# Turning the feed-forward activations outside TensorE: blocks on VectorE, an exchange by ScalarE

## The reference

```python
def swiglu_ffn(x, w_gu, w_down):
    a, u = jnp.split(x @ w_gu, 2, axis=-1)
    return (jax.nn.silu(a) * u) @ w_down

x = layer_norm(DEEPNORM_ALPHA * x + 0.5 * swiglu_ffn(x, ffn1_w_gu[l], ffn1_w_down[l]), ln1_g[l], ln1_b[l])
```

## Time and profile before

| | us |
|---|---|
| median of three runs | 1330.7 (1329.37, 1330.7, 1332.88) |
| span of the profiled execution, first to last instruction | 1328.9 |
| PE busy in it | 1311.6 |
| DVE busy | 1019.8 |
| ACT busy | 675.3 |
| POOL busy | 105.4 |

### The profile page before, as it was taken

One profiled execution on the slowest core, in us unless ns is written; L12 is line 12 of the kernel. 1 busy time (PEld: TensorE's weight loads), 2 busy tenths in 40 slices (PEclk: granted clock), 3 DMA queues, 4 the chain that ended last, 5 costly groups with the idle time before them and its releaser, 6 DMA issues.

```text
span 1328.9 us, 18838 instructions
## 1 busy us (share of the span) xinstructions
PE 1311.6 (99%) x7096; PEld 1110.0 (84%) x7096; DVE 1019.8 (77%) x1625; ACT 675.3 (51%) x1069; POOL 105.4 (8%) x153
## 2 busy tenths in 40 slices
PE   9999999999999999999999999999999999999997
PEld 7888888788888888888887888888889998798995
DVE  6677778887777677777787887778676798966986
ACT  6444444644444344444446545444436667457672
POOL 1010100011011001111010011111000000000000
PEclk9999999999999999999999999999999999999999
DMA  8977756527767656776646358777646473463630
GB/s 268 326 232 229 226 187 208 142 96 246 244 228 233 222 185 219 223 236 228 236 161 202 102 173 292 231 253 235 221 142 200 146 237 129 143 214 118 203 128 32
DMA packets 195049, 264.92 MB, mean 199 GB/s; under 512 B 17232, under 2 KB 140240, under 8 KB 194448
## 3 DMA queue, kind: packets, MB, share of 16 engines
q1 hardware_dynamic: 183248, 223.12, 52.1%
q0 software_dynamic: 11712, 40.60, 8.9%
HBM read 262.61 MB, written 1.07 MB: 198 GB/s over the span
## 4 chain that ended last, share of the span: by engine, by line
PE 87%; DVE 7%; DMA 4%; ACT 1%; issue 1%; SPq 0%; DVEq 0%; ACTq 0%
PE ps L818 26%; PE ps L820 26%; PE ps L819 26%; PE ps L902 4%; DVE w_lo L1317 2%; DMA w_raw<-in_ffn_w_gu 2%; PE ps L1049 2%; DMA w_raw<-in_w_in 1%; PE ps L1084 1%; PE ps L1110 1%; DVE few_first L1346 1%; ACT w_hi L1141 1%; DVE y L1345 1%; PE ps L1018 0%; PE ps L1096 0%
## 5 line engine op out<-in xcount | busy, mean ns | idle before, releaser
L1317 DVE TENSOR_TENSOR w_lo<-w_raw,w_hi 128x1024 fp32r<-128x1024 f32 (+2 forms) x420 | 496.9, 1213 | 128.5 <-ACT w_hi L1141 126.5
L1141 ACT ACTIVATE w_hi<-w_raw 128x1024 fp32r<-128x1024 f32 (+2 forms) x420 | 431.0, 1053 | 247.9 <-DMA w_raw<-in_ffn_w_gu 122.0
L818 PE MATMUL ps<-w_hi,col_hi 128*128 128x512 f32 (+2 forms) x1024 | 396.7, 387 | 3.6 <-DVE w_lo L1324 1.4
L820 PE MATMUL ps<-w_hi,col_lo 128*128 128x512 f32 (+2 forms) x1024 | 392.0, 383 | 0.0
L819 PE MATMUL ps<-w_lo,col_hi 128*128 128x512 f32 (+2 forms) x1024 | 391.9, 383 | 0.0
L818 PEld LDWEIGHTS ps<-w_hi,col_hi 128*128 128x128 f32 x1024 | 192.6, 188 | 44.0 <-DVE w_lo L1317 4.3
L820 PEld LDWEIGHTS ps<-w_hi,col_lo 128*128 128x128 f32 x1024 | 192.5, 188 | 38.2
L819 PEld LDWEIGHTS ps<-w_lo,col_hi 128*128 128x128 f32 x1024 | 192.5, 188 | 34.6
L818 PE MATMUL ps<-w_hi,lat_hi 128*128 128x512 f32 (+2 forms) x544 | 208.8, 384 | 0.0
L820 PE MATMUL ps<-w_hi,lat_lo 128*128 128x512 f32 (+2 forms) x544 | 206.5, 380 | 0.0
L819 PE MATMUL ps<-w_lo,lat_hi 128*128 128x512 f32 (+2 forms) x544 | 206.3, 379 | 0.0
(11 more groups left out here) (148 smaller groups left out, 1172.8 us busy)
## 6 DMA issues: line engine op xcount, KB each, us to landing
w_raw<-in_ffn_w_gu SPq DMA_DIRECT2D x352, 256.0 KB, 4.5
w_raw<-in_w_in SPq DMA_DIRECT2D x108, 512.0 KB, 4.6
w_raw<-in_ffn_w_down SPq DMA_DIRECT2D x88, 512.0 KB, 4.9
mod<-in_w_ada POOLq DMA_DIRECT2D x32, 768.0 KB, 7.6
w_raw<-in_w_out SPq DMA_DIRECT2D x24, 512.0 KB, 4.5
norm_g<-in_ln_g POOLq DMA_DIRECT2D x8, 512.0 KB, 4.2
norm_b<-in_ln_b POOLq DMA_DIRECT2D x8, 512.0 KB, 6.1
w_raw<-in_w_out SPq DMA_DIRECT2D x16, 256.0 KB, 4.5
```

The source lines that it names most:

```text
L818: pe.matmul(dst, a_hi, b_hi, start=start, stop=False)
L820: return pe.matmul(dst, a_lo, b_hi, start=False, stop=stop)
L1141: act.activation(half_of(w_hi[j], n, h), half_of(raw[j], n, h), ACT.Copy).then_inc(hi_ready, 1)
L1317: tt(half_of(w_lo[j], n, h), half_of(raw[j], n, h), half_of(w_hi[j], n, h).bitcast(F32), ALU.subtract)\
```

## The change

The job `ht` is kept for the last round alone (round 10). For rounds 0 to 9 of each feed-forward stage it becomes three jobs:

- `hturn:r`, behind `gu:r:1`: VectorE transposes the 32x32 blocks of `hidden` (128x512 in one instruction) into a new buffer `h_blocks`. A block's contents are turned then, but it lies in the wrong group of 32 partitions.
- `hmove:r`, in the middle of `gu:r+1:1` (`hmove:0` of stage 0 stands just ahead of `gu:1:1`; that of stages 2, 3 and 5 in the middle of `gu:2:0`, so that round 2 holds two): ScalarE copies the 16 pieces of 32 partitions x 128 columns to where they belong, into a new buffer `h_cols`.
- `hparts:r`, behind `gu:r+2:0` (for round 9: in the tail, behind `down:7:0`): ScalarE copies the high part to `lat_hi` in two instructions of 128x256, VectorE subtracts in two.

`h_blocks` and `h_cols` have two buffers each. `down:r` waits for `hparts:r` instead of `ht:r`, and `hidden` may be overwritten when `hturn` of two rounds before is done. The core of the diff:

```diff
+    blocks, moved, parts = (lambda r, kind=kind: [(kind, s, r)] for kind in ("hturn", "hmove", "hparts"))
...
     for r in range(2, ROUNDS):
-        jobs += gu(r, 0) + [("ht", s, r - 1)]
+        jobs += gu(r, 0)[:1] + (moved(0) if r == 2 and s > 0 else []) + stored(r - 1) + gu(r, 0)[1:] + parts(r - 2)
...
-        jobs += gu(r, 1)
+        jobs += gu(r, 1)[:1] + moved(r - 1) + gu(r, 1)[1:]
+        if r < ROUNDS - 1:
+            jobs += blocks(r)
...
-    jobs += down(tail[0], 0) + down(tail[1], 0) + [("ht", s, ROUNDS - 1)] + down(tail[2], 0) + down(tail[3], 0)
+    jobs += down(tail[0], 0) + parts(ROUNDS - 2) + down(tail[1], 0) + [("ht", s, ROUNDS - 1)] + down(tail[2], 0) + down(tail[3], 0)
...
                 elif kind == "down":
                     r, i = job[2:]
-                    turns_done(("ht", s, r))
+                    if r < ROUNDS - 1:
+                        pe.wait_ge(h_split, at["hparts", (s, r)])
+                    else:
+                        turns_done(("ht", s, r))
...
+                elif kind == "hmove":
+                    r = job[2]
+                    act.wait_ge(h_turned, at["hturn", (s, r)])
+                    if at["hturn", (s, r)] > 2:
+                        act.wait_ge(h_split, at["hturn", (s, r)] - 2)
+                    for b in range(4):
+                        for a in range(4):
+                            act.activation(h_cols[32 * b:32 * b + 32, r % 2, a, :], h_blocks[32 * a:32 * a + 32, r % 2, b, :], ACT.Copy)\
+                                .then_inc(h_moved, 1)
+                elif kind == "hparts":
...
+                    act.activation(h_part(lat_hi, q)[:, 0], h_as_columns[:, r % 2, 0], ACT.Copy)
+                    act.activation(h_part(lat_hi, q)[:, 1], h_as_columns[:, r % 2, 1], ACT.Copy).then_inc(hi_part, 1)
...
+                elif kind == "hturn":
...
+                    dve.transpose(h_blocks[:, r % 2, :, :].rearrange("p b (c t) -> p b c t", t=32),
+                                  hidden[:, r % 2, :, :].rearrange("p i (g b f) -> p b (i g) f", g=2, b=4)).then_inc(h_turned, 1)
+                elif kind == "hparts":
...
+                    dve.wait_ge(hi_part, at["hi_part", job])
+                    tt(h_part(lat_lo, q)[:, 0], h_as_columns[:, r % 2, 0], h_part(lat_hi, q)[:, 0].bitcast(F32), ALU.subtract)
+                    tt(h_part(lat_lo, q)[:, 1], h_as_columns[:, r % 2, 1], h_part(lat_hi, q)[:, 1].bitcast(F32), ALU.subtract)\
+                        .then_inc(h_split, 1)
```

More of the change, by code:

```diff
@@ L165, in ffn_jobs @@
     down = lambda r, i: [("down", s, r, i)]
+    blocks, moved, parts = (lambda r, kind=kind: [(kind, s, r)] for kind in ("hturn", "hmove", "hparts"))
+    stored = lambda r: []
     if s == 0:
@@ L169, in ffn_jobs @@
         jobs += gu(0, 1)[:1] + first((6, 7)) + [("xt", s, 1, 1)] + gu(0, 0)[1:] + gu(0, 1)[1:]
-        jobs += gu(1, 0)[:1] + [("ht", s, 0)] + gu(1, 0)[1:] + [("params", s)] + gu(1, 1)
+        jobs += blocks(0) + gu(1, 0)[:1] + stored(0) + gu(1, 0)[1:] + [("params", s)] + moved(0) + gu(1, 1) + blocks(1)
     else:
         jobs = gu(0, 0)[:1] + halves(s, ("gu", 1, 1)) + gu(0, 0)[1:] + gu(1, 0)[:1] + xt(s, 1) + halves(s, ("gu", 2, 0))
-        jobs += gu(1, 0)[1:] + gu(0, 1) + [("params", s)]
-        jobs += gu(1, 1)[:1] + [("ht", s, 0)] + gu(1, 1)[1:]
+        jobs += gu(1, 0)[1:] + gu(0, 1) + blocks(0) + [("params", s)]
+        jobs += gu(1, 1)[:1] + stored(0) + gu(1, 1)[1:] + blocks(1)
     lag = 0
     for r in range(2, ROUNDS):
-        jobs += gu(r, 0) + [("ht", s, r - 1)]
+        jobs += gu(r, 0)[:1] + (moved(0) if r == 2 and s > 0 else []) + stored(r - 1) + gu(r, 0)[1:] + parts(r - 2)
         if r > 2:
@@ L453, in count_jobs @@
                     ENDS["sums", s, tile] = ENDS[group]
-        if kind in ("xt", "ht", "trlat", "ycols"):
+        if kind in ("xt", "ht", "hparts", "trlat", "ycols"):
             COUNT.add("hi_part", job)
+        if kind in ("hturn", "hparts"):
+            COUNT.add(kind, job[1:])
+        if kind == "hmove":
+            COUNT.add(kind, job[1:], 16)
         if kind == "ycols" and not TURN[job]:
@@ L640, in build @@
         hidden = arena[:, 512:1536].rearrange("p (r t n) -> p r t n", r=2, t=TT)
+        h_blocks = arena[:, 1536:2560].rearrange("p (r b n) -> p r b n", r=2, b=4)
+        h_cols = arena[:, 2560:3584].rearrange("p (r a n) -> p r a n", r=2, a=4)
         rows1 = arena[:, 0:TT * IN1].rearrange("p (t n) -> p t n", t=TT)
@@ L747, in sink_of, with h_part @@
             return sinks.rearrange("p (f j) -> p f j", f=2)[:, :, pairs[0]:pairs[-1] + 1]
+        def h_part(tile, q):
+            return tile[:, q:q + 2, :].rearrange("p g (i a t) -> p g i a t", i=TT, a=4)
+        h_as_columns = h_cols.rearrange("p r a (i g t) -> p r g i a t", i=TT, g=2)
         def sum_banks(s, i):
@@ L1191, in _ @@
                         .then_inc(hi_part, 1)
+                elif kind == "hmove":
[8 more added lines that the diff above has]
+                elif kind == "hparts":
+                    r = job[2]
+                    q = 2 * (r % 4)
+                    act.wait_ge(h_moved, at["hmove", (s, r)])
+                    if r >= 4:
+                        act.wait_ge(used, NUMBER[s, ("down", r - 4)] + 1)
+                    act.activation(h_part(lat_hi, q)[:, 0], h_as_columns[:, r % 2, 0], ACT.Copy)
+                    act.activation(h_part(lat_hi, q)[:, 1], h_as_columns[:, r % 2, 1], ACT.Copy).then_inc(hi_part, 1)
                 elif kind == "T":
@@ L1405, in _ @@
                         ALU.mult, ALU.mult).then_inc(hidden_done, 1)
+                elif kind == "hturn":
+                    r = job[2]
+                    dve.wait_ge(hidden_done, at["hidden", (s, r, 1)])
+                    if at["hturn", (s, r)] > 2:
+                        dve.wait_ge(h_moved, 16 * (at["hturn", (s, r)] - 2))
+                    dve.transpose(h_blocks[:, r % 2, :, :].rearrange("p b (c t) -> p b c t", t=32),
+                                  hidden[:, r % 2, :, :].rearrange("p i (g b f) -> p b (i g) f", g=2, b=4)).then_inc(h_turned, 1)
+                elif kind == "hparts":
+                    r = job[2]
+                    q = 2 * (r % 4)
+                    dve.wait_ge(hi_part, at["hi_part", job])
+                    tt(h_part(lat_lo, q)[:, 0], h_as_columns[:, r % 2, 0], h_part(lat_hi, q)[:, 0].bitcast(F32), ALU.subtract)
+                    tt(h_part(lat_lo, q)[:, 1], h_as_columns[:, r % 2, 1], h_part(lat_hi, q)[:, 1].bitcast(F32), ALU.subtract)\
+                        .then_inc(h_split, 1)
                 elif kind == "ht":
```

9 lines of the change are left out of this document (5 added, 4 removed).

## The result

The changed kernel takes 1351.9 us (median of 1347.79, 1351.70, 1352.05 and 1352.14) against 1330.4 for the kernel before on the same chip: the ratio is 1.0151, with a 95% interval from 1.014 to 1.0163. It is 21.5 us slower; 1318 was forecast, 1314 to 1329 the range. The profiled execution has a span of 1350.2 us, against 1328.9, and a mean granted TensorE clock of 0.988, against 0.998.

A forecast was written before the change was run, and what follows sets the result against it. TensorE, busy 1311.6 of 1328.9 us, was taken as the bound. Removed turns −17.6, stalls +4.0 in tails, +0.5 in stage 5, +0.5 at stage 0's start: −12.6, so 1330.7 becomes 1318.1; range 1314 to 1329.

The forecast's parts named there:

- Removed: 40 x 0.44 us: TensorE, ten rounds in each of four stages: forty turns of four transposes go, 0.44 us each, 17.6 us in all.
- VectorE: Middle rounds: a block transpose of 0.7 us and split subtractions add 0.85 us, hidden in 3.8 us of idling a round.
- ScalarE: "0.297 − 0.11 = 0.19 a copy": Exchange of each round: copies of 0.297 us overlap by 0.11, so 16 take 3.0 us, 3.1 with the last one's end.
- the prediction's own sign of being wrong: Profile of ScalarE's exchange: copies over 0.3 us from start to start would show the forecast wrong.
- rival of longer copies: ScalarE's 32-partition copies take 0.39 us each, adding 3.1 us at seven places; time 1340, slower; chance 0.11.
- The tail: End of every stage: `down:9:0` waits for the second subtraction of `hparts:9`; TensorE stands 1.0 us, 4.0 in four stages.
- Round 2 of stage 5: Round holding two `hmove`: parts ready at 824.9, `down:0:0` wants to start at 824.35; TensorE stands 0.5 us.
- Stages 2 and 3, called even: Round 2 there: the same sum as in stage 5 comes out even, as TensorE's silu is later against ScalarE.
- The start of stage 0: At `gu:3:1`: the low part's chain begins at a transfer and does not move with TensorE, which stands 0.5 us.
- the rival's formula: Longer-copies rival: extra exchange time counts whole in four tails and round 2 of stages 2, 3, 5, added to 5.0 us.
- no change: Whole kernel: within about 0.3%, 4 us, of the time before; its rival has the gain go back, 1329; chance 0.15.

The follow-up runs named there:

- round 4 of the first forms: Changed kernel with some rounds' exchanges replaced by 16 copies in other forms; round 4 copied partition group 0 to group 0 each time: 0.20 us a copy.

## Why the prediction was wrong

- **Removed: 40 x 0.44 us.** Right. The timelines show 0.43 to 0.46 us at all turns but one, where a wait went with the turn, and 0.41 net in a middle round.
- **VectorE.** Right: a block transpose takes 0.711 us and is hidden; in the four middle rounds above TensorE has no gap.
- **ScalarE: "0.297 − 0.11 = 0.19 a copy".** This is the step that failed. The duration was right and the overlap was not: it was read from pairs of copies that both start at partition 0, and a copy that starts in another group of partitions does not overlap. It is 0.33 instead of 0.19, 2.2 us for each exchange, and past the prediction's own sign of being wrong, 0.3 from start to start. Its rival of longer copies, priced up to 0.39 and given 0.11, had the way from the copies to the stalls, but not the cause: it suspected the form with 32 partitions, which costs nothing by itself (round 4 of the first forms). What it set against that, that "every pair of plain copies in the rows overlaps", was true of the rows, but none of them changes its group.
- **The tail.** Right in its links, and in size but for the copies: 1.0 + 2.2 = 3.2, and 3.4 was measured.
- **Round 2 of stage 5.** The same: 0.5 + 2.2 = 2.7, and 2.70 was measured; with copies of 0.20 it was 0.84, so part of the agreement is luck. Stages 2 and 3, called even, stall too: 0.5 to 0.6 with copies of 0.20, 3.1 and 3.3 with those of 0.33.
- **The start of stage 0.** Wrong place and size. 0.5 us was expected at `gu:3:1`; instead `hparts:0`, moved past a weight split that waits for its transfer, holds up `down:0:0` for 3.0 us even with no copies. The trace of before had this wait of ScalarE, 4.64 us ahead of 44.18; the prediction did not ask what was moved behind it.
- **A term that was missing: the clock.** By the rival's formula, 5.0 + 7 x 2.2 = 20.4 us of stalls, the kernel would have taken 1333, which the prediction counted as no change. The remaining 19 are 5.9 more of stalls (3.0 in stage 0, 2.0 in stages 2 and 3) and 12.7 behind seven of the eight, where TensorE ran at half speed. The prediction had no term for time lost behind a stall, and gave no reason for leaving it out.

By single runs the way from the forecast to the result is this: from 1318 to 1325.3 with copies that overlap (mostly stage 0's wait and its clock), to 1341.2 with the real copies and the clock held up, and to 1351.9 with its fall.

## What to carry to other kernels

An overlap read from the trace holds for the form it was read from: before a loop of many small instructions is priced by it, measure the pair that the loop will really make, here two copies from different groups of partitions. Work that hides in the middle of a stage is dear at its ends: changing only the rounds with slack gained 11.9 of the 17.6 us, and changing all lost 21.5. When work is moved, look at every wait of the engine that it is moved past; and price a stall of TensorE not by its length alone, as here half as much again followed it.

## What was not expected of the hardware

- ScalarE copies of 128 columns start 0.20 us apart, whether on 32, 64 or 128 partitions and whether to the same or to another group, and 0.33 apart where the group differs from that of the copy before; with 256 columns and a change of group it is 0.44.
- Behind stalls of 2.7 to 3.5 us TensorE fell to half its clock in seven of eight cases, and in the eighth (the tail of stage 3, 3.41 us) it did not; nor did it behind the 2.99 us in the run without the exchange, while it did behind 2.94 us with the copies in one group. What decides between them was not tried.
- GpSimd copies 32x128 from one group to another in 0.29 us alone, 0.35 from start to start; beside VectorE's subtractions of 128x1024 it takes four times that.
